# Merge and output projection of a decoder layer: fp32 products replaced by three split fp32r products each, weights streamed in 128-column tiles

## What is computed

```python
m = (gm[:, :, 0] * (o_a.astype(x.dtype) @ lp['w_br_a'])
     + gm[:, :, 1] * (o_b @ lp['w_br_b'])
     + gm[:, :, 2] * (o_c.astype(x.dtype) @ lp['w_br_c']))
mix = m.astype(x.dtype) @ lp['w_o']
x = layer_norm(DEEPNORM_ALPHA * x + g_m * mix, lp['ln1_g'], lp['ln1_b'])
```

## Time and profile before

| | |
|---|---|
| median of 3 runs | 2797.47 us (2796.63, 2797.47, 2809.92) |
| the profiled execution's own time | 2810.91 us |
| its span, from the first to the last instruction | 2809.1 us |
| mean granted PE clock over the span | 0.832 |
| PE busy | 2036.8 us |
| DVE busy | 1357.4 us |
| ACT busy | 442.3 us |

### The profile page before, as it was taken

One profiled execution on the slowest core, in us unless ns is written; L12 is line 12 of the kernel. 1 busy time (PEld: TensorE's weight loads), 2 busy tenths in 40 slices (PEclk: granted clock), 3 DMA queues, 4 the chain that ended last, 5 costly groups with the idle time before them and its releaser, 6 DMA issues. The chain is left out here.

```text
span 2809.1 us, 38178 instructions
## 1 busy us (share of the span) xinstructions
PE 2036.8 (73%) x16050; PEld 1729.2 (62%) x16050; DVE 1357.4 (48%) x2126; ACT 442.3 (16%) x976; POOL 310.0 (11%) x350
## 2 busy tenths in 40 slices
PE   4986889789921002999959988127777976999995
PEld 2985778788910002899956566013435856999994
DVE  2135666665305533666605665454572346444444
ACT  1242333222200000000004454001111000000000
POOL 0000000000021212122003454004120000000000
PEclk7997999999965555999955898558878997999997
DMA  7434313122466863333139900127245103233220
GB/s 233 126 103 121 84 44 81 47 71 79 122 217 168 163 127 115 117 128 127 37 128 326 313 33 1 36 64 269 95 147 214 48 1 87 87 91 89 80 66 32
DMA packets 291913, 317.20 MB, mean 113 GB/s; under 512 B 92573, under 2 KB 246934, under 8 KB 287135
## 3 DMA queue, kind: packets, MB, share of 16 engines
q1 hardware_dynamic: 263998, 215.82, 26.2%
q0 software_dynamic: 24320, 79.94, 9.1%
q10 hardware_dynamic: 3424, 19.01, 2.1%
HBM read 287.10 MB, written 79.71 MB: 131 GB/s over the span
## 5 line engine op out<-in xcount | busy, mean ns | idle before, releaser
L307 PE MATMUL inp_acc<-hh,inp_wh 128*128 128x272 f32 (+1 forms) x1072 | 342.9, 320 | 32.6 <-DVE inp_wl L279 18.6
L307 PE MATMUL inp_acc<-hh,inp_wl 128*128 128x272 f32 (+1 forms) x1072 | 316.6, 295 | 0.0
L307 PE MATMUL inp_acc<-hl,inp_wh 128*128 128x272 f32 (+1 forms) x1072 | 316.2, 295 | 0.0
L307 PEld LDWEIGHTS inp_acc<-hh,inp_wh 128*128 128x128 f32 (+1 forms) x1072 | 207.9, 194 | 55.0 <-issue 27.7
L279 DVE TENSOR_TENSOR inp_wl<-inp_w,inp_wh 128x1024 fp32r<-128x1024 f32 (+1 forms) x67 | 81.2, 1213 | 268.4 <-ACT inp_wh L459 267.9
L307 PEld LDWEIGHTS inp_acc<-hl,inp_wh 128*128 128x128 f32 (+1 forms) x1072 | 208.5, 195 | 3.5 <-issue 3.1
L307 PEld LDWEIGHTS inp_acc<-hh,inp_wl 128*128 128x128 f32 (+1 forms) x1072 | 207.7, 194 | 0.5
L288 PE MATMUL ffn_acc<-ffn_hh,ffn_wh 128*128 128x272 f32 x704 | 147.3, 291 | 36.4 <-DVE ffn_wl L279 36.4
L1355 PE MATMUL cmp_pH<-cmp_RTh,cmp_w1h 128*128 128x256 f32 (+1 forms) x576 | 171.1, 297 | 2.7 <-issue 2.7
L1355 PE MATMUL cmp_pH<-cmp_RTh,cmp_w1l 128*128 128x256 f32 (+1 forms) x576 | 167.7, 291 | 3.0 <-issue 3.0
L1355 PE MATMUL cmp_pH<-cmp_RTl,cmp_w1h 128*128 128x256 f32 (+1 forms) x576 | 168.1, 292 | 2.0 <-issue 2.0
(11 more groups left out here) (443 smaller groups left out, 4109.1 us busy)
## 6 DMA issues: line engine op xcount, KB each, us to landing
inp_w<-in_w_in_dram SPq DMA_DIRECT2D x66, 512.0 KB, 4.3
out_dram<-in_cache_dil_dram SPq DMA_DIRECT2D x1, 32704.0 KB, 152.7
ffn_w<-in_w_ffn_dram SPq DMA_DIRECT2D x60, 512.0 KB, 4.0
sdi_w<-in_w_ada_dram ACTq DMA_DIRECT2D x8, 2048.0 KB
PT<-inp_o SPq DMA_DIRECT2D x58, 272.0 KB
sdi_kv<-in_cache_dil_dram POOLq DMA_DIRECT2D x36, 256.0 KB, 12.2
sdi_kv<-in_cache_dil_dram SPq DMA_DIRECT2D x36, 256.0 KB
ada_wada<-in_w_ada_dram SPq DMA_DIRECT2D x8, 1024.0 KB, 9.3
```

The source lines that it names most:

```text
L307: i = pe.matmul(out, l, r, start=(first and n == 0), stop=(last and n == 2))
```

## The change

Both groups of products are made as three fp32r products. The branch activations are split once at the start of the block (`xh` by ACT, `xl` by DVE), merged activations by DVE as they arise (`mh`, `ml`). Weights come in 16 tiles of 128 columns, 8 of ten chunks (640 KB, three transfers) and 8 of `w_o` (512 KB, one transfer), into three buffers `w`; ACT makes the high part `wh`, DVE the low part `wl`, in two buffers each. SP loads `xT` after the gates of tile 2. PE begins the output projection when the branch sums are taken and waits chunk by chunk for merged tiles (`merged`) in its first tile.

```diff
-        wb = sb("wb", [P, 10, D])
-        wo = sb("wo", [P, KD, D])
+        w = sb("w", [P, 3, NB, P])
+        wh, wl = sb("wh", [P, 2, NB, P], F32R), sb("wl", [P, 2, NB, P], F32R)
+        xh, xl = sb("xh", [P, NB, NT], F32R), sb("xl", [P, NB, NT], F32R)
+        mh, ml = sb("mh", [P, KD, NT], F32R), sb("ml", [P, KD, NT], F32R)
...
+                def load(i):
+                    if i >= 3:
+                        sp.wait_ge(wlow, i - 2)
...
+                for n in range(KD):
+                    load(n)
+                    gates(n)
+                    if n == 2:
+                        for k in range(KD):
+                            sp.dma_start(m["xT"][:, k, :], saved_rows(a, k)).then_inc(xloaded, 16)
+                for n in range(KD):
+                    load(KD + n)
 
             @block.scalar
             def _(act):
+                def weights(i):
+                    act.wait_ge(loaded[i % 3], arrived(i))
+                    if i >= 2:
+                        act.wait_ge(done if i < KD + 2 else out, 3 * (i - 1) if i < KD + 2 else i - KD - 1)
+                    nc.scalar.activation(wh[:, i % 2, 0:chunks(i)], w[:, i % 3, 0:chunks(i)], ACT.Copy).then_inc(whigh, 1)
+
+                at = 0
+                for _, src, nk in BR:
+                    nc.scalar.activation(xh[:, at:at + nk, :], m[src][:, :, :], ACT.Copy).then_inc(xhigh, 1)
+                    at += nk
+                    if at == 4:
+                        weights(0)
                 for n in range(KD):
                     act.wait_ge(gl[n % 2], 48 * (n // 2 + 1))
                     nc.scalar.activation(gt[:, 3 * (n % 2):3 * (n % 2) + 3, :], gt[:, 3 * (n % 2):3 * (n % 2) + 3, :], ACT.Sigmoid).then_inc(sig, 1)
+                    weights(n + 1)
+                for i in range(KD + 1, 2 * KD):
+                    weights(i)
...
-                pe.wait_ge(loaded, 48)
                 for n in range(KD):
                     at = 0
+                    pe.wait_ge(wlow, n + 1)
                     for b, (_, src, nk) in enumerate(BR):
...
                         for k in range(nk):
-                            for h in range(2):
-                                i = pe.matmul(acc[:, w % 4, h, 0:HN], wb[:, at + k, n * P:(n + 1) * P],
-                                              m[src][:, k, h * HN:(h + 1) * HN], start=(k == 0), stop=(k == nk - 1))
+                            i = split_product(pe, acc[:, u % 4], (wh[:, n % 2, at + k], wl[:, n % 2, at + k]),
+                                              (xh[:, at + k], xl[:, at + k]), k == 0, k == nk - 1)
                         i.then_inc(done, 1)
                         at += nk
-                pe.wait_ge(wol, 16)
-                pe.wait_ge(used, 3 * KD)
                 for n in range(KD):
+                    pe.wait_ge(wlow, KD + n + 1)
+                    pe.wait_ge(used, 3 * KD)
                     if n >= 4:
                         pe.wait_ge(oused, n - 3)
                     for k in range(KD):
-                        for h in range(2):
-                            i = pe.matmul(acc[:, n % 4, h, 0:HN], wo[:, k, n * P:(n + 1) * P], mT[:, k, h * HN:(h + 1) * HN],
-                                          start=(k == 0), stop=(k == KD - 1))
+                        if n == 0:
+                            pe.wait_ge(merged, k + 1)
+                        i = split_product(pe, acc[:, n % 4], (wh[:, n % 2, k], wl[:, n % 2, k]), (mh[:, k], ml[:, k]), k == 0, k == KD - 1)
                     i.then_inc(out, 1)
...
                 for n in range(KD):
+                    weights(n + 1)
                     dve.wait_ge(sig, n + 1)
...
+                    c(dve.tensor_tensor(t1[:, :], t1[:, :], t2[:, :], ALU.add))
+                    c(split_high(dve, mh[:, n], t1[:, :]))
+                    c(split_low(dve, ml[:, n], t1[:, :], mh[:, n]))
+                    dve.sem_inc(merged, 1)
+                dve.wait_ge(xloaded, 16 * KD)
                 for n in range(KD):
+                    if n + 1 < KD:
+                        weights(KD + n + 1)
                     dve.wait_ge(out, n + 1)
```

More of the change, by code:

```diff
@@ L1547, in merge @@
     BR = (("w_br_a", "oaT", 4), ("w_br_b", "obT", 4), ("w_br_c", "ocT", 2))
+    NB = 10
     with ExitStack() as ctx:
         sem, sb, ps = (f(nc, ctx, "mrg") for f in (sem_maker, sb_maker, ps_maker))
-        wb = sb("wb", [P, 10, D])
-        wo = sb("wo", [P, KD, D])
+        w = sb("w", [P, 3, NB, P])
+        wh, wl = sb("wh", [P, 2, NB, P], F32R), sb("wl", [P, 2, NB, P], F32R)
+        xh, xl = sb("xh", [P, NB, NT], F32R), sb("xl", [P, NB, NT], F32R)
+        mh, ml = sb("mh", [P, KD, NT], F32R), sb("ml", [P, KD, NT], F32R)
         gt = sb("gt", [P, 6, NT])
@@ L1555, in merge, with arrived @@
         acc = ps("acc", [P, 4, 2, 512])
-        mT = sb("mT", [P, KD, NT])
-        loaded, xl, wol, sig, done, used, ch, out, oused = (sem(s) for s in ("loaded", "xl", "wol", "sig", "done", "used", "ch", "out", "oused"))
+        xloaded, xhigh, xlow, whigh, wlow, sig, done, used, ch, out, oused, merged = (
+            sem(s) for s in ("xl", "xhigh", "xlow", "whigh", "wlow", "sig", "done", "used", "ch", "out", "oused", "merged"))
         gl = [sem(f"g{i}") for i in range(2)]
+        loaded = [sem(f"w{i}") for i in range(3)]
+        def arrived(i):
+            return 16 * sum(3 if j < KD else 1 for j in range(i % 3, i + 1, 3))
+        chunks = lambda i: NB if i < KD else KD
         with nc.Block() as block:
@@ L1562, in _, with gates @@
             def _(sp):
[L1563 to L1569, removed]
+                def load(i):
+                    if i >= 3:
+                        sp.wait_ge(wlow, i - 2)
+                    n = i % KD
+                    if i >= KD:
+                        sp.dma_start(w[:, i % 3, 0:KD, :], a["w_o"][0].rearrange("(k p) n -> p k n", p=P)[:, :, n * P:(n + 1) * P]).then_inc(loaded[i % 3], 16)
+                        return
+                    at = 0
+                    for name, _, nk in BR:
+                        sp.dma_start(w[:, i % 3, at:at + nk, :],
+                                     a[name][0].rearrange("(k p) n -> p k n", p=P)[:, :, n * P:(n + 1) * P]).then_inc(loaded[i % 3], 16)
+                        at += nk
+                def gates(n):
                     if n >= 2:
@@ L1574, in _ @@
                         sp.dma_start(gt[:, 3 * (n % 2) + b, :], a["PT"][t * P:(t + 1) * P, :]).then_inc(gl[n % 2], 16)
-                    if n == 1:
-                        sp.dma_start(wo[:, :, :], a["w_o"][0].rearrange("(k p) n -> p k n", p=P)).then_inc(wol, 16)
+                for n in range(KD):
[6 more added lines that the diff above has]
+                    load(KD + n)
             @block.scalar
             def _(act):
+                def weights(i):
[3 more added lines that the diff above has]
+                    nc.scalar.activation(wh[:, i % 2, 0:chunks(i)], w[:, i % 3, 0:chunks(i)], ACT.Copy).then_inc(whigh, 1)
+                at = 0
+                for _, src, nk in BR:
+                    nc.scalar.activation(xh[:, at:at + nk, :], m[src][:, :, :], ACT.Copy).then_inc(xhigh, 1)
+                    at += nk
+                    if at == 4:
+                        weights(0)
                 for n in range(KD):
@@ L1582, in _ @@
                     nc.scalar.activation(gt[:, 3 * (n % 2):3 * (n % 2) + 3, :], gt[:, 3 * (n % 2):3 * (n % 2) + 3, :], ACT.Sigmoid).then_inc(sig, 1)
+                    weights(n + 1)
+                for i in range(KD + 1, 2 * KD):
+                    weights(i)
             @block.tensor
             def _(pe):
-                pe.wait_ge(loaded, 48)
                 for n in range(KD):
                     at = 0
+                    pe.wait_ge(wlow, n + 1)
                     for b, (_, src, nk) in enumerate(BR):
-                        w = 3 * n + b
-                        if w >= 4:
-                            pe.wait_ge(used, w - 3)
+                        u = 3 * n + b
+                        if n == 0:
+                            pe.wait_ge(xlow, b + 1)
+                        if u >= 4:
+                            pe.wait_ge(used, u - 3)
                         for k in range(nk):
-                            for h in range(2):
-                                i = pe.matmul(acc[:, w % 4, h, 0:HN], wb[:, at + k, n * P:(n + 1) * P],
-                                              m[src][:, k, h * HN:(h + 1) * HN], start=(k == 0), stop=(k == nk - 1))
+                            i = split_product(pe, acc[:, u % 4], (wh[:, n % 2, at + k], wl[:, n % 2, at + k]),
+                                              (xh[:, at + k], xl[:, at + k]), k == 0, k == nk - 1)
                         i.then_inc(done, 1)
                         at += nk
-                pe.wait_ge(wol, 16)
-                pe.wait_ge(used, 3 * KD)
                 for n in range(KD):
+                    pe.wait_ge(wlow, KD + n + 1)
+                    pe.wait_ge(used, 3 * KD)
```

(24 more changed lines are left out.)

## The result

The changed kernel takes 2773.49 us (median of 6 runs, 2762.49 to 2781.45) against 2802.76 us before in the same comparison: a ratio of 0.9893, 95% interval [0.9866, 0.9919], 29 us or 1.1% less. Two more comparisons gave 0.9897 [0.9868, 0.9927] and 0.9878 [0.9854, 0.9901]. The forecast was 32.4 us less, 2765 us; of the 8.5 us between 2765 and 2773.5, 5.3 are the kernel before, which was 2797.5 us in the runs that the forecast started from. The gain of 29.3 us lies halfway between the 32.4 of the forecast and the 26.5 of the rival with late early tiles (2771), and 2773.5 just outside the forecast's own range (2758 to 2773), inside the whole range; the time alone does not decide between the two, the profile has to.

What follows compares the result with a forecast made beforehand. PE was taken to bound the merge block; products 24.5, start 7.9, half clock 0.5 and output projection 0.9, less 1.4 for the xT wait, gave 32.4 us. Forecast 2765 us against the median, range 2752 to 2784.

Steps and rivals of the forecast that it cites:

- the rival with late early tiles: Early merge tiles: xT or DVE's queue runs late, 5 to 7 us of the gain go, 2771 us; chance 0.20.
- the whole range: Run time of the kernel: 2752 to 2784 us, covering shorter spacing, late tiles and a median on the upper level.
- Products, 24.5 us: PE's branch and output products: 864 fp32r matmuls at 0.125 us replace 576 records at 0.230, 24.5 us less.
- The rival with a shorter spacing: PE's matmuls: 0.116 us each in place of 0.125, 8 us more gained, 2757 us; chance 0.06.
- Start, 7.9 us: Block start: PE's first product at +7.7 after weight tile 0 and its two splits, 7.9 us earlier than +15.6.
- Half clock at the start: PE's first sum: 24 matmuls at half clock cost 2.5 us, against 3.0 before, so 0.5 us gained.
- The wait at tile 3: Branch tile 3: xT ahead on SP delays its low part to +34.1, so PE waits 1.4 us.
- The bound from the issue of xT: Upper bound of the tile 3 wait: 5 us if the xT issues take 10.1 us, as behind the big weights.
- Steady tiles: Branch tiles: 7.5 us each on PE, DVE busy about 6.7, low part ready with 3 us to spare.
- Output projection: Start of the output projection: PE waits 0.85 us for the last branch sums, 1.74 before; 0.9 us gained.
- What follows … keeps its own length: Behind the block: normalisation and feed forward wait for the last product and take as long as before.
- The slower one: All weight tiles: each over 4 us late with the clock falling, about 2848 us; chance 0.05.

Runs made afterwards that it cites:

- e3_stream_fp32: Changed kernel with streamed weights kept but all splits removed and fp32 products again; ratio to before 0.995, block 184.5 us.
- e1_spread: Changed kernel with one xT load behind the gates of each of the 8 tiles; ratio to before 0.987, block 160.7 us.
- e1_again: Repeat of e1_spread on the same chip as a_third and e6_pieces; ratio to before 0.9873, block 164.1 us.
- e4_two_products: Changed kernel without the product of low weights with high activations, four matmuls a chunk for six; one run, block 147.4 us.
- e2_xt_first: Changed kernel with all eight xT loads ahead of weight tile 0; one run, block 167.7 us.
- e6_pieces: e1_spread with weight tile 0 awaited and split in three pieces, both large activations made high first; ratio to before 0.9869, block 161.0 us.
- a_third: Changed kernel, unedited, on the same chip as e1_again and e6_pieces; ratio to before 0.9878, block 164.3 us.
- a_again: Changed kernel once more, no edit, beside the kernel before; ratio to before 0.9897, block 165.0 us.
- e5_dve_both: Changed kernel with DVE making the weights' high parts too, ACT only those of activations; ratio to before 0.9917, block 165.2 us.

## Why the prediction was right, point by point

- **Products, 24.5 us.** Right. 0.126 us a matmul, and the difference between e3_stream_fp32 and e1_spread gives 23.7 us once the start and its clock are taken out. The rival with a shorter spacing, 0.116 us, did not come: 384 matmuls took 48.4 us. The Trainium skill, page "TensorE: Matmul & The Clock Gate", section "Wait — 56ns, not 53.3ns?", gives back-to-back matmuls the columns over 2.4 GHz plus 2.5 ns, from which 0.116 us is an estimate; this trace, with 0.126, does not agree.
- **Start, 7.9 us.** Right: +7.4 to +8.3 in the six executions whose start is made so (the changed kernel three times, e1_spread, e1_again, e4_two_products), forecast +7.7. e2_xt_first made the weights arrive later and e6_pieces waited for fewer of them, and the first product moved with it.
- **Half clock at the start.** The step "which costs 24 × (0.229 − 0.125) = 2.5 us" was taken from the 5.5 us of the earlier trace rows. Measured: 2.9 us at half clock, a cost of 1.3 us. In other executions with the same start it was 2.8 (a_third), 3.2 (e1_spread), 3.9 (a_again) and 6.2 us (e1_again), so the earlier trace rows were one draw of several. The 1.2 us gained here were worth nothing at the end: PE came earlier to tile 3, whose low part was no earlier, and waited the longer.
- **The wait at tile 3.** The mechanism was right (e1_spread removes it), and the moment as well: the low part was forecast at +34.1 and was done at +34.5. The wait was 2.6 us and not 1.4, because PE was there 0.7 us sooner than forecast, after the shorter half clock, and the low part 0.4 later. The bound from the issue of xT (10.1 us behind the large weights) was rightly left: here it took 4.5 us.
- **What follows that wait.** This term was missing from the sum. I gave a clock loss only to waits near 4.3 us, from "A wait of 3.7 us left the clock at 1.00, one of 4.3 us was followed by 3.2 us at 0.50". Waits of 2.6, 1.9 and 1.75 us at tile 3 were each followed by some 3 to 4 us at half clock, about 1.6 us lost.
- **Steady tiles.** Right: 7.51 us a branch tile, no other wait, DVE close behind. The low part of tile 6 was done 2.7 us before PE took it, 3 forecast. e4_two_products measured DVE's pace as 6.9 us (forecast 6.7), e5_dve_both 7.8 (forecast 7.6).
- **Output projection.** Right: PE waits 1.0 us ahead of it (forecast 0.85) and no more, 48.4 us for eight tiles.
- **"What follows … keeps its own length".** Wrong by 1.6 us in this pair of profiles: the normalisation's first sum took 9.2 us in place of 7.6 for its clock.

Together: the last product's reader was forecast at +120.5 and came at +123.3, 2.8 us late. Tile 3 began 0.4 late, the half clock behind its wait cost 1.6, the step to the output projection 0.4 and its eight tiles 0.4 (48.4 us against 48.0). With the 1.6 us of the normalisation the forecast 32.4 become 28.0, which is what the block measured. The median gained 29.3 us; that it lies above 28.0 is within its interval and says nothing more. Of the rivals, early tiles late came nearest: its mechanism, a wait followed by half clock, is there at tile 3, and at no other tile, with 2.6 us in place of its 5. The slower one needed the same at each tile and met it at one of sixteen.

## What to carry to other kernels

Count a change in one block from that block's first instruction: here the two profiles differ by 48 us, of which 28 lie in the changed block. When fp32 products are replaced by three fp32r ones, price them by spacing (0.229 us × 4 against 0.125 us × 6 for a chunk of 544 columns) and then add up the vector engine's work for each tile, since the splits put it within 10% of being the limit (6.9 us of 7.5). A block of transfers that nobody needs soon, in one queue ahead of one that is needed at once, delays that one by its own transfer time: 5.8 us here, of which 1.75 to 2.6 us showed as a wait, with some 1.6 us of half clock behind it. Spread over the loop they cost no wait; a gain in the time of a run was not shown.

## What the hardware showed that I had not expected

Short waits cost more clock than the trace before suggested, and not in a fixed way. At tile 3 waits of 1.75, 1.9 and 2.6 us were all followed by half clock; in e4_two_products waits of 1.3 to 1.7 us at four tiles, three of them in a row, were not, and in e5_dve_both a wait of 1.3 us at tile 3 was not, but one of 2.9 us ahead of the output projection was. In the runs with no wait at tile 3 (e1_spread twice, e2_xt_first, e3_stream_fp32, e6_pieces) the clock stayed at 1.00 from its first rise to the end of the products. Ahead of the normalisation PE is idle for 3.7 to 3.8 us in every kernel, and the first sum behind it took 7.6 us (before and e5_dve_both), 9.2 to 9.3 (the changed kernel, three times, e1_spread, e2_xt_first, e4_two_products) or 10.3 to 10.5 us (e1_again, e3_stream_fp32, e6_pieces). So the same idle time costs between 0 and 2.9 us. What decides it was not tried; it is of the size of the improvements that e1_spread and e6_pieces make, and hides them.
